# A third k-tile pair by the seven-product scheme, with its weight sums moved from VectorE to GpSimd

## The chip, the cores and the metric

One NeuronCore of a Trainium2 chip runs the kernel. The metric is the device time of one execution in microseconds (us), given as the median of several runs; lower is better. Engines are named as in the profile: PE is TensorE, DVE is VectorE, ACT is ScalarE, POOL is GpSimd, SP is SyncE, which here only issues DMAs.

## What is computed

One layer of a hybrid encoder, on 256 tokens with a model width of 2048, all in float32. Only the two feed-forward blocks (width 5632) are touched by the change:

```
h = h + 1/2 * ((silu(u @ w_gate) * (u @ w_up)) @ w_down),   u = rms_norm(h)
```

One stands ahead of the attention part and one behind it. Between them lie a combined projection, a forgetting attention, a gated linear attention, a merge and an output projection; at the end come a per-layer embedding and a last norm. The weights are far larger than the activations, so every weight is read once and streamed.

## The kernel before

**Precision.** Each float32 matrix is split into a high part (rounded by ACT with a copy, the fp32r type) and a low part (raw minus high, by DVE). A product is three matmuls: high x high, high x low, low x high (`product`, L1511). Each matmul is 128x128 activations against 128x512 weights.

**Phases.** Each feed-forward block is cut into an "a" and a "b" half: `up1a`, `down1a`, `up1b`, `down1b` for the first, `up2a`, `down2a`, `up2b`, `down2b` for the second. The phase before `up2a` is `out`. In an up phase the work goes by column pairs (a stage for each, `pair`): 256 hidden columns of gate beside 256 of up in each of two 512-column tiles. A stage has the 2048 rows of k as 16 k-tiles, taken two at a time: 8 units. `UPS` (L47) gives the pairs of each phase: 5, 5, 6 and 5 stages.

**Items.** A unit done plainly is an item of kind S: 2 column tiles x 2 k-tiles x 2 token tiles x 3 = 24 matmuls. The first `US` = 2 units of a pair (but not of a phase's first pair) are done by Winograd's form of the seven-product scheme: on the 2x2 blocks of the unit, 7 products instead of 8. Four of them (kind A, 12 matmuls) are made in the stage of the pair before, three (kind B, 9 matmuls) in the pair's own stage. Between A and B the banks are combined: ACT copies two banks (`copy_parts`, L632), DVE makes four additions (`combine`, L1072), and PE waits for `combined` before the stage (L1555).

The scheme needs sums of activations (`make_sums`, L1082, once for each feed-forward block, in the first stage of the "a" half) and four sums of weight tiles for every A item: `make_steps` (L1062), on DVE:

```
q[1] = q[2] - q[0];  q[2] = b[1] - q[2];  q[3] = b[1] - q[1];  b[2] = b[0] - q[3]
```

Each is 128x512 with both inputs in SBUF. `q` is the raw buffer of the A item (four tiles, one "quad"), `b` the "trio" that holds the rest of the unit until its B item in the next stage.

**Buffers and order.** There are `QUADS` = 3 raw quads, 3 high and 3 low quads. `stage_of` (L58) writes out the order of a stage:

```
own = [("B", pair, 0), own[US], ("B", pair, 1), *own[US + 1:]]      # L62
own = [*own[:-2], *later, *own[-2:]]                                 # L65
```

so B0 S2 B1 S3 S4 S5 A0 A1 S6 S7. `item_tables` (L108) works out for each item the count at which its buffers are free. SP issues the loads in that order (L393 to L403): it waits on `lo_split` for the raw quad, then issues 1 MB for an S item, or two loads of 512 KB for an A item, with a wait for the trio between them. ACT makes the high part (`split_item`, L620) after a wait for the load (or for `steps_made`) and for PE's item three before (`quad_free`); DVE makes the low part (L1053); PE multiplies (`multiply_item`, L1517). Every engine works in its own program order, and after certain items the engines do other work: the silu and the products of the last pair after the second item (k == 1), their turns into rows after the third on PE and the fifth on ACT and DVE.

One raw quad lies in `more(name)`: for `up2a` and `up2b` in the space of `x_both`, which the phase before `up2a` still reads. So SP waits for the whole `out` phase at L392 before it issues any load of `up2a`.

**POOL** makes constants at the start, the roots of the norms (`root`, L455), small DMAs and, in the merge phase, `bias_scores` (L510): two additions, 128x128 and 128x256, with both inputs in SBUF, for each of eight heads. It does nothing in the feed-forward blocks but the roots.

Of the kernel before, what the change touches and what calls it, by code (L numbers as in the profile page):

```python
# [8 lines left out]
P = 128  # L9
# [6 lines left out]
TOK = 256  # L16
# [33 lines left out]
US = 2  # L50
# [92 lines left out]
def build(nc, x, x_turned, all_gains, p, ffn1_up, ffn1_w_down, w_in,  # L143
# [36 lines left out]
    with ExitStack() as ctx:  # L180
# [29 lines left out]
        room, room_r = shared(("room", [P, 9, COLS], F32), ("room_r", [P, 9, COLS], F32R))  # L210
# [4 lines left out]
        later_in_chunk = sb("later_in_chunk", [P, P])  # L215
        up_to = sb("up_to", [P, P])
        ones = sb("ones", [P, P])
        causal = sb("causal", [P, 3 * P])
# [13 lines left out]
        thin_rows = sb("thin_rows", [P, TOK])  # L232
# [29 lines left out]
        def trio(name, u):  # L262
            return more(name)[0][:, 12:15, :] if u == 0 else room[:, 4:7, :]

        def spare(name):
            return more(name)[0][:, 15, :]

        s_hi = room_r[:, 0:2, :].rearrange("p u (s c) -> p u s c", s=4)
        s_lo = room_r[:, 2:4, :].rearrange("p u (s c) -> p u s c", s=4)
        m1_copy, m5_copy = room[:, 7, :], room[:, 8, :]  # L270
# [32 lines left out]
        steps_made, parts_copied, combined = sem("steps_made"), sem("parts_copied"), sem("combined")  # L303
# [57 lines left out]
        def _(sp):  # L361
# [11 lines left out]
            def feed_forward(up, w_up, first_pair, w_down, kt0, kts):  # L373
# [17 lines left out]
                if up == "up2a":  # L391
                    sp.wait_ge(multiplied, BLOCK[up])  # L392
                for stage in STAGES[up]:  # L393
                    for it in stage:
                        source = w_up[first_pair + it.pair, it.unit]
                        if it.kind != "B" and it.raw_free > 0:
                            sp.wait_ge(lo_split, it.raw_free)
                        if it.kind == "S":
                            sp.dma_start(raw_quad(up, it.raw), source).then_inc(quad_full[it.raw], 16)
                        if it.kind == "A":  # L400
                            sp.dma_start(raw_quad(up, it.raw)[:, 0:3:2, :], source[:, 0:2, :]).then_inc(quad_full[it.raw], 16)
                            sp.wait_ge(lo_split, it.trio_free)
                            sp.dma_start(trio(up, it.unit)[:, 0:2, :], source[:, 2:4, :]).then_inc(trio_full[it.unit], 16)  # L403
# [45 lines left out]
        def _(pool):  # L449
# [9 lines left out]

            nc.gpsimd.memset(ident[:], 0.0).then_inc(pool_chain, 1)  # L460
# [3 lines left out]
            nc.gpsimd.memset(minus_half[:], -0.5).then_inc(ident_ready, 1)  # L464
            nc.gpsimd.memset(ones[:], 1.0).then_inc(pool_chain, 1)
# [16 lines left out]
            root(0)  # L482
            pool.wait_ge(multiplied, BLOCK["down1b"])
# [59 lines left out]
            root(2)  # L543

# [14 lines left out]
        def _(act):  # L559
# [60 lines left out]
            def split_item(name, it):  # L620

                n = 3 if it.kind == "B" else 4
                of = trio(name, it.unit) if it.kind == "B" else raw_quad(name, it.raw)
# [5 lines left out]
                nc.scalar.activation(hi_quad(name, it.quad)[:, 0:n, :], of[:, 0:n, :], ACT.Copy)\  # L629
                    .then_inc(hi_split, item_counts(name, it))  # L630
# [11 lines left out]
            def split_sums(first):  # L642
                for u in range(US):
                    act.wait_ge(sums_made, first + u + 1)
                    nc.scalar.activation(s_hi[:, u, :, :], (m1_copy, m5_copy)[u].rearrange("p (s c) -> p s c", s=4), ACT.Copy)\
# [345 lines left out]
        def _(dve):  # L991
# [61 lines left out]
            def split_item(name, it):  # L1053

                n = 3 if it.kind == "B" else 4
                of = trio(name, it.unit) if it.kind == "B" else raw_quad(name, it.raw)
                dve.wait_ge(hi_split, it.at + 1)
                nc.vector.tensor_tensor(lo_quad(name, it.quad)[:, 0:n, :], of[:, 0:n, :],  # L1058
                                        hi_quad(name, it.quad)[:, 0:n, :].bitcast(F32), ALU.subtract)\
                    .then_inc(lo_split, item_counts(name, it))  # L1060

            def make_steps(name, it):  # L1062

                dve.wait_ge(quad_full[it.raw], 16 * it.raw_count)
                dve.wait_ge(trio_full[it.unit], 16 * it.trio_count)
                q, b = raw_quad(name, it.raw), trio(name, it.unit)
                after_own(nc.vector.tensor_tensor(q[:, 1, :], q[:, 2, :], q[:, 0, :], ALU.subtract))
                nc.vector.tensor_tensor(q[:, 2, :], b[:, 1, :], q[:, 2, :], ALU.subtract)
                after_own(nc.vector.tensor_tensor(q[:, 3, :], b[:, 1, :], q[:, 1, :], ALU.subtract))
                nc.vector.tensor_tensor(b[:, 2, :], b[:, 0, :], q[:, 3, :], ALU.subtract).then_inc(steps_made, 1)  # L1070

            def combine(name, pair):  # L1072
# [3 lines left out]
                u2 = spare(name)  # L1076
                after_own(nc.vector.tensor_tensor(u2, c22[:, :], m1_copy, ALU.add))
                nc.vector.tensor_tensor(c12[:, :], c12[:, :], u2, ALU.add)
                after_own(nc.vector.tensor_tensor(c21[:, :], c21[:, :], u2, ALU.add))
                nc.vector.tensor_tensor(c22[:, :], c21[:, :], m5_copy, ALU.add).then_inc(combined, 1)  # L1080

            def make_sums(name, hi, lo, sums):  # L1082

                for u in range(US):
                    full = spare(name).rearrange("p (k c) -> p k c", k=2)
                    to = (m1_copy, m5_copy)[u].rearrange("p (s c) -> p s c", s=4)
                    pair_of = slice(BK * u, BK * (u + 1))
                    after_own(nc.vector.tensor_tensor(full, hi[:, pair_of, :].bitcast(F32), lo[:, pair_of, :].bitcast(F32), ALU.add))
# [5 lines left out]
                    dve.wait_ge(sums_made, sums + u + 1)  # L1094

            def split_sums(first):
                for u in range(US):
                    dve.wait_ge(sums_hi, first + u + 1)
                    nc.vector.tensor_tensor(s_lo[:, u, :, :], (m1_copy, m5_copy)[u].rearrange("p (s c) -> p s c", s=4),
                                            s_hi[:, u, :, :].bitcast(F32), ALU.subtract).then_inc(sums_lo, 1)  # L1100

            def up_groups(name, kts, sums=None, hi=None, lo=None, first_rows=None, later_rows=None):

                pairs, first = UPS[name]
                for n, stage in enumerate(STAGES[name]):
                    pair = first + n
                    for k, it in enumerate(stage):
                        if k + 1 < len(stage) and stage[k + 1].kind == "A":
                            make_steps(name, stage[k + 1])
                        split_item(name, it)  # L1110
                        if k == 0 and n == 0 and first_rows:
                            first_rows()
                        if k == 1 and pair > 0:
                            hidden_out(name, pair - 1)
                        if k == 1 and n == 0:
                            if later_rows:
                                later_rows()
# [809 lines left out]
```

## Time and profile before

| | |
|---|---|
| Median of 3 runs | 2248.66 us (2248.65 to 2249.57) |
| Profiled execution | 2249.12 us, of which the span from first to last instruction is 2247.1 us |
| Mean granted clock of PE | 0.995 |
| Busy | PE 99%, DVE 60%, ACT 47%, POOL 2% |
| DMA | 425.66 MB, mean 189 GB/s |

The profile lists a matmul with about 0.39 us, but matmuls are pipelined: the distance between two starts is what one costs. A group's line gives busy time and the mean of one instruction. An idle time in brackets is that just before the instruction, with what ended it. "L1058" is the line of the kernel.

### The profile page before, as it was taken

The numbers are of one execution on the slowest core, as the hardware profiler recorded it, in microseconds if no ns is written. First come the engines' busy times: TensorE is split into PE (matmuls) and PEld (weight loads), VectorE is DVE, ScalarE is ACT, GpSimd is POOL, SyncE is SP. The second block draws the span as 40 slices with busy tenths as digits, with TensorE's granted clock in tenths as the row PEclk, the third lists the DMA queues.
The fourth block names the chain that finished last, engine by engine and source line by source line (L and its number), as shares of the span: only waits on it lengthen the run. The fifth ranks groups of instructions, "written<-read, shape, count | busy, mean of one in ns | idle before, by whom it ended". The sixth has DMA issues, their size and how long they took to land.

```text
span 2247.1 us, 24310 instructions
## 1 busy us (share of the span) xinstructions
PE 2217.0 (99%) x9950; PEld 1827.4 (81%) x9950; DVE 1337.5 (60%) x1318; ACT 1050.7 (47%) x1147; POOL 40.4 (2%) x71
## 2 busy tenths in 40 slices
PE   8999999999999999999999998899999999999998
PEld 7888888888888888877778887788878888888886
DVE  5777544677555444445655654777754467755555
ACT  6445434454444444464444443454543345544454
POOL 0000000000010000010000000000000000000000
PEclk9999999999999999999999999999999999999999
DMA  8455456555465666665655664555546664556654
GB/s 312 177 202 205 164 196 205 207 186 191 175 201 187 198 195 190 175 179 173 174 168 159 187 187 143 213 172 203 207 149 191 204 221 171 197 178 212 187 189 147
DMA packets 161079, 425.66 MB, mean 189 GB/s; under 512 B 11320, under 2 KB 11328, under 8 KB 143568
## 3 DMA queue, kind: packets, MB, share of 16 engines
q1 hardware_dynamic: 159216, 419.21, 57.3%
q0 software_dynamic: 1472, 4.70, 0.8%
q8 instruction: 74, 1.21, 0.2%
q10 hardware_dynamic: 288, 0.30, 0.0%
q14 instruction: 29, 0.24, 0.0%
HBM read 422.06 MB, written 2.11 MB: 189 GB/s over the span
## 4 chain that ended last, share of the span: by engine, by line
PE 97%; DMA 1%; DVE 1%; ACT 0%; issue 0%; ACTq 0%; POOLq 0%; POOL 0%
PE acc L1470 18%; PE acc L1472 18%; PE acc L1471 18%; PE acc L1513 6%; PE acc L1515 6%; PE acc L1514 6%; PE turn L1515 4%; PE turn L1513 4%; PE turn L1514 4%; PE fox L1515 4%; PE fox L1514 4%; PE fox L1513 4%; DMA raw<-in_ffn_up 1%; PE turn L1490 1%; PE acc L1507 0%; PE turn L1762 0%
## 5 line engine op out<-in xcount | busy, mean ns | idle before, releaser
L1003 DVE TENSOR_TENSOR w_lo<-raw,w_hi 128x1024 fp32r<-128x1024 f32 x451 | 557.9, 1240 | 604.0 <-ACT w_hi L573 603.6
L573 ACT ACTIVATE w_hi<-raw 128x1024 fp32r<-128x1024 f32 x451 | 477.0, 1060 | 704.0 <-PE acc L1472 633.9
L1470 PE MATMUL acc<-w_hi,x_both 128*128 128x512 f32 x940 | 370.7, 394 | 2.8 <-DVE x_both L1165 2.8
L1472 PE MATMUL acc<-w_hi,x_both 128*128 128x512 f32 x940 | 366.3, 390 | 0.0
L1471 PE MATMUL acc<-w_lo,x_both 128*128 128x512 f32 x940 | 365.9, 389 | 0.0
L1470 PE MATMUL acc<-w_hi,slab_r 128*128 128x512 f32 x832 | 325.9, 392 | 2.6 <-DVE w_lo L1003 2.6
L1472 PE MATMUL acc<-w_hi,slab_r 128*128 128x512 f32 x832 | 324.5, 390 | 0.0
L1471 PE MATMUL acc<-w_lo,slab_r 128*128 128x512 f32 x832 | 324.4, 390 | 0.0
L1058 DVE TENSOR_TENSOR w_lo<-raw,w_hi 128x2048 fp32r<-128x2048 f32 x84 | 192.2, 2290 | 100.8 <-ACT w_hi L629 100.3
L629 ACT ACTIVATE w_hi<-raw 128x2048 fp32r<-128x2048 f32 x84 | 161.2, 1919 | 191.1 <-PE fox L1515 93.5
L1470 PEld LDWEIGHTS acc<-w_hi,x_both 128*128 128x128 f32 x940 | 176.5, 188 | 44.8 <-issue 5.7
L1472 PEld LDWEIGHTS acc<-w_hi,x_both 128*128 128x128 f32 x940 | 176.4, 188 | 37.5
L1471 PEld LDWEIGHTS acc<-w_lo,x_both 128*128 128x128 f32 x940 | 176.6, 188 | 35.3
L1470 PEld LDWEIGHTS acc<-w_hi,slab_r 128*128 128x128 f32 x832 | 156.6, 188 | 34.9 <-issue 2.9
L1472 PEld LDWEIGHTS acc<-w_hi,slab_r 128*128 128x128 f32 x832 | 156.6, 188 | 32.8
L1471 PEld LDWEIGHTS acc<-w_lo,slab_r 128*128 128x128 f32 x832 | 156.5, 188 | 32.2
L1058 DVE TENSOR_TENSOR w_lo<-more,w_hi 128x2048 fp32r<-128x2048 f32 (+1 forms) x41 | 87.4, 2132 | 46.4 <-ACT w_hi L629 46.3
L629 ACT ACTIVATE w_hi<-more 128x2048 fp32r<-128x2048 f32 (+1 forms) x41 | 73.5, 1794 | 72.5 <-PE fox L1515 36.6
L629 ACT ACTIVATE more_r<-more 128x2048 fp32r<-128x2048 f32 (+1 forms) x34 | 63.1, 1856 | 53.9 <-PE acc L1515 30.0
L1058 DVE TENSOR_TENSOR more_r<-more,more_r 128x2048 fp32r<-128x2048 f32 (+1 forms) x34 | 75.2, 2211 | 20.2 <-ACT more_r L629 20.0
L1513 PE MATMUL acc<-w_hi,y_r 128*128 128x512 f32 x183 | 72.9, 398 | 9.3 <-DVE w_lo L1058 9.3
L1058 DVE TENSOR_TENSOR more_r<-raw,more_r 128x2048 fp32r<-128x2048 f32 x26 | 59.5, 2290 | 28.0 <-ACT more_r L629 27.9
(368 smaller groups left out, 3200.9 us busy)
## 6 DMA issues: line engine op xcount, KB each, us to landing
raw<-in_ffn_up SPq DMA_DIRECT2D x88, 1024.0 KB, 4.9
raw<-in_ffn_w_down SPq DMA_DIRECT2D x176, 512.0 KB
raw<-in_w_in SPq DMA_DIRECT2D x96, 512.0 KB
more<-in_ffn_up SPq DMA_DIRECT2D x46, 1024.0 KB, 4.9
raw<-in_w_merge_gate SPq DMA_DIRECT2D x64, 512.0 KB
raw<-in_ffn_up SPq DMA_DIRECT2D x37, 512.0 KB, 4.0
raw<-in_w_out SPq DMA_DIRECT2D x32, 512.0 KB
raw<-in_w_ple_gate SPq DMA_DIRECT2D x32, 512.0 KB
```

Source lines behind the costliest of these rows:

```text
L573: nc.scalar.activation(w_hi[:, slot, :, :], raw[:, slot, :, :], ACT.Copy).then_inc(hi_split, 1)
L629: nc.scalar.activation(hi_quad(name, it.quad)[:, 0:n, :], of[:, 0:n, :], ACT.Copy)\
L1003: nc.vector.tensor_tensor(w_lo[:, slot, :, :], raw[:, slot, :, :], w_hi[:, slot, :, :].bitcast(F32), ALU.subtract).then_inc(lo_split, 1)
L1058: nc.vector.tensor_tensor(lo_quad(name, it.quad)[:, 0:n, :], of[:, 0:n, :], hi_quad(name, it.quad)[:, 0:n, :].bitcast(F32), ALU.subtract)\
L1470: nc.tensor.matmul(to, hi(kt)[:, tok], w_hi[:, slot, k, :], start=kt == 0, stop=False)
L1471: nc.tensor.matmul(to, hi(kt)[:, tok], w_lo[:, slot, k, :], start=False, stop=False)
L1472: last = nc.tensor.matmul(to, lo(kt)[:, tok], w_hi[:, slot, k, :], start=False, stop=kt == BK * nb - 1)
L1490: last = nc.tensor.transpose(turn_bank[bank][:, at:at + P], tile(k, tok), ident[:])
L1513: nc.tensor.matmul(to, x, w, start=start, stop=False, skip_group_check=primed)
L1514: nc.tensor.matmul(to, x, w_rest, start=False, stop=False, skip_group_check=primed)
L1515: return nc.tensor.matmul(to, x_rest, w, start=False, stop=stop, skip_group_check=primed)
```

## The change

- `US` goes from 2 to 3, so three of eight units of a pair are done with seven products, in 17 pairs.
- The order of a stage becomes B0 S3 B1 S4 A0 B2 S5 A1 S6 A2 S7, and in a phase's first stage S0 S1 S2 S3 A0 S4 S5 A1 S6 A2 S7.
- `make_steps` moves from DVE to POOL, which waits for its own results by a semaphore; POOL runs through all A items of two phases (`all_steps`). The making of constants moves behind `up1b`, and the trio of the third unit uses the space of constants ("corner"), so its B item is split in two instructions on ACT and on DVE.
- `make_sums` and `split_sums` use one buffer for the sums of all three units, so that a unit's sums are split before the next one's are made; they come after the third item (k == 2).
- `copy_parts` and `combine` move from the end of a stage to behind the first item of the next one.
- SP's wait for the end of `out` moves to the third item of `up2a`.

```diff
-US = 2
+US = 3
@@ stage_of
-        own = [("B", pair, 0), own[US], ("B", pair, 1), *own[US + 1:]]
+        b0, b1, b2 = [("B", pair, u) for u in range(US)]
+        own = [b0, own[US], b1, own[US + 1], b2, *own[US + 2:]]
     if pair + 1 < pairs:
-        later = [("A", pair + 1, u) for u in range(US)]
-        own = [*own[:-2], *later, *own[-2:]]
+        a0, a1, a2 = [("A", pair + 1, u) for u in range(US)]
+        own = [*own[:4], a0, *own[4:6], a1, own[6], a2, own[7]]
@@ build
+        corner = sb("corner", [P, 2 * COLS])
-            return more(name)[0][:, 12:15, :] if u == 0 else room[:, 4:7, :]
+            return more(name)[0][:, 12:15, :] if u == 0 else room[:, 8:11, :]
+        def later_tiles(name, u):
+            if u < 2:
+                return (trio(name, u),)
+            return corner.rearrange("p (a c) -> p a c", a=2), more(name)[0][:, 15:16, :]
-        m1_copy, m5_copy = room[:, 7, :], room[:, 8, :]
+        m1_copy, m5_copy = room[:, 6, :], room[:, 7, :]
@@ SP
-                if up == "up2a":
-                    sp.wait_ge(multiplied, BLOCK[up])
                 for stage in STAGES[up]:
                     for it in stage:
+                        if up == "up2a" and it.at == BLOCK[up] + 2:
+                            sp.wait_ge(multiplied, BLOCK[up])
@@ POOL
+            def after_step(ins):
+                steps[0] += 1
+                ins.then_inc(step_chain, 1)
+                pool.wait_ge(step_chain, steps[0])
+            def make_steps(name, it):
+                pool.wait_ge(quad_full[it.raw], 16 * it.raw_count)
+                pool.wait_ge(trio_full[it.unit], 16 * it.trio_count)
+                q, later = raw_quad(name, it.raw), later_tiles(name, it.unit)
+                w21, w22 = later[0][:, 0, :], later[0][:, 1, :]
+                t4 = later[0][:, 2, :] if len(later) == 1 else later[1][:, 0, :]
+                after_step(nc.gpsimd.tensor_tensor(q[:, 1, :], q[:, 2, :], q[:, 0, :], ALU.subtract))
+                nc.gpsimd.tensor_tensor(q[:, 2, :], w22, q[:, 2, :], ALU.subtract)
+                after_step(nc.gpsimd.tensor_tensor(q[:, 3, :], w22, q[:, 1, :], ALU.subtract))
+                nc.gpsimd.tensor_tensor(t4, w21, q[:, 3, :], ALU.subtract).then_inc(steps_made, 1)
...
+            root(0)
+            all_steps("up1a")
+            all_steps("up1b")
+            pool.wait_ge(multiplied, BLOCK["down1b"])
             nc.gpsimd.memset(ones[:], 1.0).then_inc(pool_chain, 1)
...
             root(2)
+            all_steps("up2a")
+            all_steps("up2b")
@@ ACT, up_phase
                         split_item(name, it)
+                        if k == 0 and n > 0:
+                            copy_parts(name, pair)
...
-                        if k == 3 and n == 0 and sums is not None:
+                        if k == 2 and n == 0 and sums is not None:
                             split_sums(sums)
...
-                    if pair + 1 < pairs:
-                        copy_parts(name, pair + 1)
@@ DVE
             def combine(name, pair):
-                u2 = spare(name)
-                after_own(nc.vector.tensor_tensor(u2, c22[:, :], m1_copy, ALU.add))
+                after_own(nc.vector.tensor_tensor(m1_copy, c22[:, :], m1_copy, ALU.add))
...
             def make_sums(hi, lo, first):
                 for u in range(US):
+                    full = m5_copy.rearrange("p (k c) -> p k c", k=2)
+                    to = m1_copy.rearrange("p (s c) -> p s c", s=4)
...
                     nc.vector.tensor_tensor(to[:, 3, :], a12, to[:, 1, :], ALU.subtract).then_inc(sums_made, 1)
                     dve.wait_ge(sums_hi, first + u + 1)
+                    nc.vector.tensor_tensor(s_lo[:, u, :, :], to, s_hi[:, u, :, :].bitcast(F32), ALU.subtract)\
+                        .then_inc(sums_lo, 1)
+                    dve.wait_ge(sums_lo, first + u + 1)
@@ DVE, up_groups
-                        if k + 1 < len(stage) and stage[k + 1].kind == "A":
-                            make_steps(name, stage[k + 1])
                         split_item(name, it)
+                        if k == 0 and n > 0:
+                            combine(name, pair)
...
-                            if sums is not None:
-                                make_sums(name, hi, lo, sums)
-                        if k == 3 and n == 0 and sums is not None:
-                            split_sums(sums)
+                        if k == 2 and n == 0 and sums is not None:
+                            make_sums(hi, lo, sums)
...
-                    if pair + 1 < pairs:
-                        combine(name, pair + 1)
```

## Rows read from the trace of the kernel before

**Rows 1.** The page, part 1: busy us of each engine (share) and instructions.
```profile
PE 2217.0 (99%) x9950; PEld 1827.4 (81%) x9950; DVE 1337.5 (60%) x1318; ACT 1050.7 (47%) x1147; POOL 40.4 (2%) x71
```

**Rows 2.** Waits of PE, whole span: us in total, times, longest.
```profile
PE acc L1513 <- DVE w_lo L1058: 9.3, 1, 9.3
PE acc L1513 <- DVE more_r L1058: 3.0, 1, 3.0
...
PE acc L1470 <- DVE w_lo L1003: 2.6, 1, 2.6
```

**Rows 3.** Timeline of one S item: PE's first matmul, the next item's, ACT after it.
```profile
401.99 0.39 PE L1513 MATMUL turn<-more_r,x_both 128*128 128x512 f32 x1
...
407.43 0.39 PE L1513 MATMUL turn<-w_hi,x_both 128*128 128x512 f32 x1
...
407.69 1.92 ACT L629 ACTIVATE more_r<-more 128x2048 fp32r<-128x2048 f32 x1 [3.52 <-PE fox L1515]
```

**Rows 4.** Chain that ended last: the turns of stages two apart (start, us).
```profile
1560.16 0.87 PE acc L1507 x8
1646.30 0.87 PE acc L1507 x8
```

**Rows 5.** Groups by form, ACT and DVE: busy us, mean ns, idle before.
```profile
L629 ACT ACTIVATE w_hi<-raw 128x2048 fp32r<-128x2048 f32 x84 | 161.2, 1919 | 191.1 <-PE fox L1515 93.5 <-PE acc L1515 64.3 <-DMA raw<-in_ffn_up 15.3
...
L1058 DVE TENSOR_TENSOR w_lo<-raw,w_hi 128x2048 fp32r<-128x2048 f32 x84 | 192.2, 2290 | 100.8 <-ACT w_hi L629 100.3
```

**Rows 6.** SP's timeline at an A load, and landing times of its second half (L403).
```profile
1957.25 0.38 SPq L401 DMA_DIRECT2D raw<-in_ffn_up  x1
1957.67 0.47 SPq L403 DMA_DIRECT2D room<-in_ffn_up  x1
...
DMA to landing us min/median/max: 4.6/4.9/6.1
```

**Rows 7.** Chain that ended last at the start of up2a (start, us).
```profile
1398.84 4.96 DMA raw<-in_ffn_up
...
1408.11 0.79 PE acc L1513
```

**Rows 8.** Windows: busy of PE, PEld, DVE, ACT, POOL; PEclk; DMA share; GB/s.
```profile
1408.00:1416.00 8.00, 7.89 (x22) 6.24 (x23) 3.45 (x4) 1.56 (x5) 0.00 (x0) 0.60 0.81 263
1423.00:1432.00 9.00, 6.02 (x27) 4.88 (x27) 8.54 (x8) 2.48 (x3) 0.00 (x0) 1.00 0.54 174
1672.00:1684.00 12.00, 9.45 (x35) 7.34 (x34) 7.43 (x9) 6.42 (x9) 0.00 (x0) 0.86 0.46 151
```

**Rows 9.** POOL's additions, lines 516 and 517: ns min/median/max.
```profile
L516 POOL TENSOR_TENSOR room<-causal,room x8: 469/474/1359, 974.8 to 1168.5; 128x128 f32<-128x128 f32 x8
...
L517 POOL TENSOR_TENSOR room<-causal,room x8: 734/741/1717, 976.1 to 1168.9; 128x256 f32<-128x256 f32 x8
```

**Rows 10.** Timelines of POOL and DVE where they run together (start, us).
```profile
974.77 1.36 POOL L516 TENSOR_TENSOR room<-causal,room 128x128 f32<-128x128 f32 x1 [2.20 <-DMA room<-cum_rows]
...
978.42 1.72 POOL L517 TENSOR_TENSOR room<-causal,room 128x256 f32<-128x256 f32 x1
...
974.58 1.23 DVE L1003 TENSOR_TENSOR w_lo<-raw,w_hi 128x1024 fp32r<-128x1024 f32 x1 [7.34 <-ACT w_hi L573]
975.73 1.28 DVE L1235 SCALAR_TENSOR_TENSOR gates<-turn,gates 128x512 f32<-128x512 f32 x2
...
1061.21 2.29 DVE L1003 TENSOR_TENSOR w_lo<-raw,w_hi 128x1024 fp32r<-128x1024 f32 x1 [0.53 <-ACT w_hi L573]
...
1062.71 0.57 POOL L507 DMA_DIRECT2D room<-cum_rows  x1 [0.30 <-POOL room L517]
```

**Rows 11.** Timelines of DVE and ACT: one unit's sums of activations.
```profile
1419.94 0.69 DVE L1088 TENSOR_TENSOR more<-y_r 128x512 f32<-128x512 f32 x1
...
1421.52 0.29 DVE L1093 TENSOR_TENSOR room<-more,room 128x128 f32<-128x128 f32 x1
...
1423.75 0.63 ACT L645 ACTIVATE room_r<-room 128x512 fp32r<-128x512 f32 x1 [0.83 <-DVE room L1093]
```

More of the change, by code:

```diff
@@ L214, in build @@
         ident = sb("ident", [P, P])
[L215 to L218, printed above, removed]
+        causal, up_to = corner[:, 0:3 * P], corner[:, 3 * P:4 * P]
+        later_in_chunk, ones, thin_rows = corner[:, 4 * P:5 * P], corner[:, 5 * P:6 * P], corner[:, 6 * P:8 * P]
         in_chunk = sb("in_chunk", [P, 2])
@@ L231, in build @@
         forget_bias = sb("forget_bias", [P, HEADS])
-        thin_rows = sb("thin_rows", [P, TOK])
         thin_z = sb("thin_z", [P, TT, 2 * THIN_FOX])
@@ L262, in trio @@
         def trio(name, u):
-            return more(name)[0][:, 12:15, :] if u == 0 else room[:, 4:7, :]
[L265 to L269, printed above, removed]
-        m1_copy, m5_copy = room[:, 7, :], room[:, 8, :]
+            return more(name)[0][:, 12:15, :] if u == 0 else room[:, 8:11, :]
[3 more added lines that the diff above has]
+            return corner.rearrange("p (a c) -> p a c", a=2), more(name)[0][:, 15:16, :]
+        s_hi = room_r[:, 0:3, :].rearrange("p u (s c) -> p u s c", s=4)
+        s_lo = room_r[:, 3:6, :].rearrange("p u (s c) -> p u s c", s=4)
+        m1_copy, m5_copy = room[:, 6, :], room[:, 7, :]
         x_t = slab[:, SLABS - KD:, :, :].rearrange("p k t c -> p k (t c)")
@@ L458, in root, with all_steps @@
                 nc.gpsimd.tensor_tensor(rstd[:], meansq[:], minus_half[:], ALU.pow).then_inc(rstd_done, 1)
+            steps = [0]
+            def after_step(ins):
[12 more added lines that the diff above has]
+                nc.gpsimd.tensor_tensor(t4, w21, q[:, 3, :], ALU.subtract).then_inc(steps_made, 1)
+            def all_steps(name):
+                for stage in STAGES[name]:
+                    for it in stage:
+                        if it.kind == "A":
+                            make_steps(name, it)
             nc.gpsimd.memset(ident[:], 0.0).then_inc(pool_chain, 1)
@@ L620, in split_item @@
             def split_item(name, it):
-                n = 3 if it.kind == "B" else 4
-                of = trio(name, it.unit) if it.kind == "B" else raw_quad(name, it.raw)
                 if it.kind == "S":
@@ L628, in split_item @@
                 act.wait_ge(multiplied, it.quad_free)
-                nc.scalar.activation(hi_quad(name, it.quad)[:, 0:n, :], of[:, 0:n, :], ACT.Copy)\
-                    .then_inc(hi_split, item_counts(name, it))
+                at = 0
+                for of in later_tiles(name, it.unit) if it.kind == "B" else (raw_quad(name, it.raw),):
+                    n = of.shape[1]
+                    last = nc.scalar.activation(hi_quad(name, it.quad)[:, at:at + n, :], of, ACT.Copy)
+                    at += n
+                last.then_inc(hi_split, item_counts(name, it))
             def copy_parts(name, pair):
@@ L644, in split_sums @@
                     act.wait_ge(sums_made, first + u + 1)
-                    nc.scalar.activation(s_hi[:, u, :, :], (m1_copy, m5_copy)[u].rearrange("p (s c) -> p s c", s=4), ACT.Copy)\
+                    nc.scalar.activation(s_hi[:, u, :, :], m1_copy.rearrange("p (s c) -> p s c", s=4), ACT.Copy)\
                         .then_inc(sums_hi, 1)
@@ L1053, in split_item @@
             def split_item(name, it):
-                n = 3 if it.kind == "B" else 4
-                of = trio(name, it.unit) if it.kind == "B" else raw_quad(name, it.raw)
                 dve.wait_ge(hi_split, it.at + 1)
[L1058 to L1070, printed above, removed]
+                at = 0
+                for of in later_tiles(name, it.unit) if it.kind == "B" else (raw_quad(name, it.raw),):
+                    n = of.shape[1]
+                    last = nc.vector.tensor_tensor(lo_quad(name, it.quad)[:, at:at + n, :], of,
+                                                   hi_quad(name, it.quad)[:, at:at + n, :].bitcast(F32), ALU.subtract)
+                    at += n
+                last.then_inc(lo_split, item_counts(name, it))
             def combine(name, pair):
@@ L1075, in combine, with make_sums @@
                 c11, c21, c12, c22 = banks_of(name, pair)
-                u2 = spare(name)
-                after_own(nc.vector.tensor_tensor(u2, c22[:, :], m1_copy, ALU.add))
-                nc.vector.tensor_tensor(c12[:, :], c12[:, :], u2, ALU.add)
-                after_own(nc.vector.tensor_tensor(c21[:, :], c21[:, :], u2, ALU.add))
+                after_own(nc.vector.tensor_tensor(m1_copy, c22[:, :], m1_copy, ALU.add))
+                nc.vector.tensor_tensor(c12[:, :], c12[:, :], m1_copy, ALU.add)
+                after_own(nc.vector.tensor_tensor(c21[:, :], c21[:, :], m1_copy, ALU.add))
                 nc.vector.tensor_tensor(c22[:, :], c21[:, :], m5_copy, ALU.add).then_inc(combined, 1)
-            def make_sums(name, hi, lo, sums):
+            def make_sums(hi, lo, first):
                 for u in range(US):
[L1085 to L1088, printed above, removed]
+                    full = m5_copy.rearrange("p (k c) -> p k c", k=2)
+                    to = m1_copy.rearrange("p (s c) -> p s c", s=4)
+                    kts = slice(BK * u, BK * (u + 1))
+                    after_own(nc.vector.tensor_tensor(full, hi[:, kts, :].bitcast(F32), lo[:, kts, :].bitcast(F32), ALU.add))
                     a11, a21, a12, a22 = full[:, 0, 0:P], full[:, 0, P:], full[:, 1, 0:P], full[:, 1, P:]
```

18 lines of the change are left out of this document (5 added, 13 removed).

## The prediction

> **What bounds the kernel now.** The page's busy row says PE 99% [rows 1]; DVE is at 60%, ACT at 47% and POOL at 2%. A busy share alone does not say that PE sets the end, so the next view is PE's waits [rows 2]: after the start-up the list holds 9.3, 3.0 and 2.6 us and nothing else. PE is therefore the bound everywhere, and a saved matmul is saved time as long as nothing comes late. The timeline gives the price: the 24 matmuls of an S item run from 401.99 to 407.43, 5.44 us, so 226.7 ns each [rows 3]; an A item (12) takes 2.72 us, a B item (9) 2.04 us. A check: the turns of two stages lie 86.14 us apart over two stages [rows 4], 43.07 us each, and 6 S + 2 A + 2 B + 0.87 us of turns is 43.03. So the stages of before have no stall at all.
>
> **What keeps them free of stalls** is a loop of latencies. There are three split buffers. ACT can begin an item's high part when PE has finished the item three before it (PE's item ends at 407.43, ACT starts at 407.69), takes 1.92 us, DVE takes 2.29 us for the low part [rows 3, 5], so the item is ready 4.5 us after that end. Raw buffers are also three: an item's load starts at the low part of the third loaded item before it. An A load is two DMAs 0.42 us apart, the second landing 4.9 us after its issue [rows 6]: 5.3 us.
>
> **The change, part by part.** (a) *Products.* A third unit in each of 17 column pairs (4+4+5+4) takes 21 matmuls for 24: 51 x 0.2267 = **-11.6 us**. A stage with A and B becomes 5 S + 3 A + 3 B + 0.87 = 42.35 us.
>
> (b) *Early loads of up2a.* SP now waits for the end of "out" before the third load only. Before, the first load is issued at 1398.84 and PE starts at 1408.1: 9.3 us idle, then a stretch at mean granted clock 0.60 for 8 us (between the 2.4 and the 1.2 GHz level), 3.2 us lost; then 3.0 us at the third item [rows 2, 7, 8]. The 2.6 us at the next hand-over (down2a's first block, whose raw slot the last item held) goes too, since 63 items end on the third buffer, and with it 14% of 12 us, 1.7 us [rows 2, 8]. Together **-19.8 us**, if nothing new stands there.
>
> (c) *Steps to POOL.* 34 x 4 DVE subtractions of 128x512 (0.69 us for one of this size [rows 11]) go, 51 x 4 POOL ones come. POOL takes 0.47 us for 128x128 and 0.74 us for 128x256 [rows 9], so 0.267 us per 128 columns and **1.28 us for 128x512**, extrapolated. Each of two waits on its own result costs 0.30 us [rows 10]. A unit's four steps: 1.28 + 0.30 + 1.23 + 1.28 + 0.30 + 1.28 = 5.7 us, where DVE took 2.7.
>
> (d) *POOL and DVE together.* The rows show that they hold each other up. The DVE split of 1.24 us takes 2.29 us when POOL's two additions run beside it; and the 0.47 us addition that meets a running split takes 1.36 us, the 0.74 us one 1.72 us [rows 10, 9]. Both sides read two SBUF operands. Two DVE operations with one input in PSUM, at 975.73, kept 0.64 us each beside POOL [rows 10], so combine, silu products and turns are taken to be free of it. I take turns, first come first served, with POOL holding for all but 0.15 us of its operation. The Trainium skill's "SBUF — State Buffer" (Who interferes with whom) states that such a pair is exclusive for the whole instruction; with that last 0.15 us held too, the sum below would be 10 us higher, and it speaks against this change as a whole. By that rule, the trace agrees on the exclusion (2.29 us for 1.24), not on the last tenths of it.
>
> (e) *One middle stage walked through*, 13 of which exist; times in us from B0's start. PE's order without stalls ends B0 2.0, S3 7.5, B1 9.5, turns 10.4, S4 15.8, A0 18.6, B2 20.6, S5 26.0, A1 28.8, S6 34.2, A2 36.9, S7 42.4. A0's second half needs the tile that B0's low part frees at -4.4, so it lands at 0.8; its steps end at 7.7 because B1's low part comes between, and S4's low part ends at 9.8. That frees A1's load, landing 15.15; steps 15.15 to 16.4 and 16.7 to 19.1. S5's high part can't start before S4's end (15.8), is ready at 18.0, its low part waits for POOL until 19.1 and ends at 21.4; PE wanted it at 20.6: **0.8**. POOL's fourth step waits for that low part, ends at 22.6; A1's low part ends at 26.8, just in time. A2's load, freed at 21.4, lands at 26.7; its first step goes ahead of S6's low part, which ends at 30.1 instead of 29.0: **0.6**. That low part in turn holds POOL's steps two and three until 30.0; step four ends at 34.1, high part 36.05, low part 38.35; PE is ready at 35.6: **2.8**. Sum 4.1 x 13 = **+54 us**. Without any exclusion only A2 is late: S5 ready 20.3, load 25.7, steps 31.3, split 35.6 against 34.2: 1.4 us.
>
> (f) *First stages.* The three sums of activations now share one copy buffer, so each waits for ACT and back: 1.87 us to the fifth operation's end, 0.63 us ACT, 0.69 us DVE and the waits, 3.4 us [rows 11], 10.2 us in a row, with S3's split behind them on ACT and DVE. In up1a they begin 4.5 us after the phase and S3's low part ends 1.9 us late, with A0's four steps on POOL in between 6.5. In up2a the third item needs the last row turns and is ready at 12.0; S3's is ready 7.6 us late, with POOL's steps 12.3. A1 and S6 of these two stages add 2.5 each, 0.2 for the third item; up1b and up2b lose 2.7 + 0.6 each. Together 9.0 + 14.9 + 3.3 + 3.3 = **+30.4 us**.
>
> (g) *Clock.* Short idles can drop it: the 2.6 us one did, the 3.0 us one did not [rows 8, 2]. For 15 stalls of about 2.8 us I take half of 1.7, 12.8 us (bounds 0 and 25); after up2a's 12.3 us the same 3.2 as before, after up1a's 6.5 some 2.5. **+18.5 us**.
>
> (h) *At nothing*: 17 more ACT and DVE instructions, since B2 is split in two (it has 5 us of room); the copies and combine, now one S item (5.44 us) before their use instead of two: 0.26 + 2 x 0.63 + 4 x 0.69 + 0.4 of waits = 4.7 us [rows 3, 11], 0.7 to spare, and one operand in PSUM; if they slip, every stage start slips. POOL's constants and thin loads move behind up1b; the constants are used 390 us later. POOL's root for up2a stays ahead of the steps there.
>
> **Sum**: -11.6 - 19.8 + 54 + 30.4 + 18.5 = **+71 us**. The profiled execution took 2249.1 us (span 2247.1), 0.4 above the median of 2248.7. **Forecast 2320 us.** Bounds: a POOL step at 1.2 instead of 1.28 us takes 9 off, at 1.35 adds 13, the clock -13 to +12.
>
> **Rivals.** *No exclusion* (8 in 100): POOL reads beside DVE. Then (e) is 13 x 1.4 = 17.8, (f) 1.9 + 7.6, clock 3.2: -11.6 - 19.8 + 17.8 + 9.5 + 3.2 = -1, **2248 us**, no change. The lengthened rows speak against it. *Faster* (5 in 100): in addition a unit's steps take under 4.3 us, that is below 0.94 us per 128x512 step; A2 is then in time, and the gain is that sum without its 17.8, -19: **2230 us**. For it: nothing but that 128x512 was never seen. *Worse* (9 in 100): DVE's queue of splits wins POOL's place more often or a step takes 1.5 us, the A2 stalls double and each drops the clock: +42 and +12, **2374 us**, against the first-come rows. *The change does not do what it says*: excluded for the products, which are counted out by the item lists; the first two up2a loads still wait for raw slots, but DVE frees these about 14 and 8 us before PE ends "out" (four slots of 2.72 us, a low part 2.6 us after its slot is free). The forecast (78 in 100) has its own range 2288 to 2355.
>
> **Range and chances.** 2265 to 2355 leaves out the faster case, no exclusion and the upper end of worse, near 2 in 10. A measurement can tell 0.2%, 4.5 us. Slower 0.90, within 0.2% 0.05, faster 0.05.
>
> **What the profile would show.** PE's waits: some 40 on DVE low parts of split items, A2's (the last A of a stage) at 2.8 us, turns of middle stages 46.5 us apart (42.4 if there are none); POOL 128x512 rows with a minimum near 1.28 us and a mean well above; DVE's 128x2048 splits lengthened from 2.29 to above 3.3 us where POOL runs; the first up2a item without its 9.3 us; a wait of 12 us at its fourth. Wrong, if POOL's rows and the DVE splits keep their minimum throughout, or if PE's waits name ACT or combine.

## The result and the profile after

| | before | after |
|---|---|---|
| Median | 2249.11 us (2248.65 to 2250.51, 4 runs) | 2320.12 us (2319.02 to 2321.19, 4 runs) |
| Ratio, 95% interval | | 1.0315 (1.0297 to 1.0332) |
| Span of the profiled execution | 2247.1 us | 2319.4 us |
| Mean granted clock of PE | 0.995 | 0.986 |

The kernel became 3.2% slower, 71 us; 2320 had been forecast. The sum was right to a microsecond, which is partly luck: its idle time was about 6 us too high and its clock about 6 us too low.

Busy times and the chain that ended last, from the page of the changed kernel (they answer to [rows 1]), and below them the chain of the kernel before:

```profile
PE 2238.3 (97%) x9899; PEld 1829.4 (79%) x9899; DVE 1341.9 (58%) x1228; ACT 1071.8 (46%) x1183; POOL 447.6 (19%) x275
...
PE 79%; DVE 6%; POOL 6%; DMA 5%; ACT 4%; issue 1%; SPq 0%; ACTq 0%; POOLq 0%; DVEq 0%
...
PE 97%; DMA 1%; DVE 1%; ACT 0%; issue 0%; ACTq 0%; POOLq 0%; POOL 0%
```

PE has 51 matmuls fewer (9899 for 9950), as counted, but it now sets only 79% of the chain, where it set 97%. The busy shares alone would mislead: PE still shows 97%. DVE has 90 instructions fewer than before, and yet its busy time did not fall (1341.9 us for 1337.5): part of what it has left takes longer, as the splits below show.

PE's waits in the changed kernel, with total us, times and the longest one (they answer to [rows 2]):

```profile
PE acc L1530 <- DVE w_lo L1093: 26.0, 14, 11.6
PE turn L1530 <- DVE more_r L1093: 19.9, 8, 7.4
PE turn L1530 <- DVE w_lo L1093: 13.9, 11, 3.1
PE acc L1530 <- DVE more_r L1093: 7.9, 8, 3.1
```

That is 67.7 us in 41 waits, all for the low part of a split item; before there were three such waits with 14.9 us. The longest, 11.6 us, is at the fourth item of `up2a`; 7.4 us is the same place in `up1a`. The other lines of PE's list are start-up waits, 4.0 us in all, where it had 6.0 before.

One middle stage on PE's timeline, from the A2 before it to its own A2:

```profile
519.02 0.80 PE L1530 MATMUL turn<-w_hi,x_both 128*128 128x512 f32 x1 [2.30 <-DVE w_lo L1093]
...
549.93 0.50 PE L1530 MATMUL turn<-w_hi,x_both 128*128 128x512 f32 x1 [0.28 <-DVE w_lo L1093]
558.65 0.50 PE L1530 MATMUL turn<-more_r,x_both 128*128 128x512 f32 x1 [0.26 <-DVE more_r L1093]
566.69 0.79 PE L1530 MATMUL acc<-w_hi,x_both 128*128 128x512 f32 x1 [2.30 <-DVE w_lo L1093]
```

The brackets give the idle time. The three waits stand where the prediction's walk had put them: at S5 (0.3 us), S6 (0.3) and A2 (2.3). From A2 to A2 it is 47.7 us, against 43.07 before [rows 4] and 42.35 without waits.

The chain that ended last, through the load and the steps of that A2:

```profile
550.33 4.68 DMA corner<-in_ffn_up
...
555.13 1.32 POOL raw L477
556.46 0.07 issue
556.52 3.22 POOL raw L478
559.74 1.26 POOL raw L479
561.00 0.07 issue
561.07 1.30 POOL more L480
562.37 0.02 issue
562.39 1.93 ACT w_hi L662
564.32 0.02 issue
564.34 2.30 DVE w_lo L1093
566.64 0.04 issue
566.69 0.79 PE acc L1530
```

Load, four steps, high part, low part, product: one after another, 16.4 us. Three POOL steps take 1.3 us; the second takes 3.22. Beside it runs the split of the item before, which takes 3.38 us instead of 2.29:

```profile
555.21 3.38 DVE L1093 TENSOR_TENSOR more_r<-more,more_r 128x2048 fp32r<-128x2048 f32 x1
```

POOL's steps and DVE's splits by duration (ns: minimum/median/maximum), from the view of single lines:

```profile
L477 POOL TENSOR_TENSOR raw<-raw x35: 1285/1439/3297, 59.7 to 2029.6; 128x512 f32<-128x512 f32 x35
...
L480 POOL TENSOR_TENSOR room<-room,raw x13: 1285/3215/3222, 93.2 to 2034.9; 128x512 f32<-128x512 f32 x13
...
L1093 DVE TENSOR_TENSOR w_lo<-raw,w_hi x93: 2279/2292/3407, 50.7 to 2082.1; 128x2048 fp32r<-128x2048 f32 x93
```

The minimum of POOL's 128x512 step is 1.285 us, where 1.28 had been extrapolated from the two smaller additions of [rows 9]. The maximum adds 1.9 to 2.0 us, most of a DVE split; the split's own maximum is 3.41 us for 2.28, most of a POOL step more. Each engine waits for the other, as in [rows 10]. Of the 168 splits of 128x2048, 41 are stretched, by 36 us in sum. A unit's four steps take POOL 5.6 to 10.6 us, 8.1 in the mean, where four plain steps and two waits would make 5.3.

Windows of 8 us behind four stalls (busy of PE, PEld, DVE, ACT, POOL; then PEclk, DMA share, GB/s), which answer to [rows 8]:

```profile
566.60:574.60 8.00, 7.91 (x28) 6.42 (x29) 5.99 (x7) 3.77 (x4) 0.00 (x0) 0.79 0.73 261
1548.00:1556.00 8.00, 8.00 (x35) 6.65 (x36) 7.58 (x7) 3.69 (x4) 0.00 (x0) 1.00 0.78 262
1594.40:1602.40 8.00, 8.00 (x29) 6.51 (x30) 6.14 (x6) 3.68 (x4) 0.00 (x0) 0.81 0.76 262
1468.80:1476.80 8.00, 7.97 (x23) 6.35 (x24) 4.37 (x2) 1.18 (x1) 0.00 (x0) 0.64 0.86 267
```

Behind 12 of the 13 A2 stalls of middle stages, each of 2.3 to 3.1 us, the mean granted clock is near 0.8 over 8 us, so about 1.6 us more are lost; the exception is the one at 1548, which with 3.09 us was among the longest. The 2.3 us stall at A2 in the first stage of `up1a` lowered nothing either. PE keeps its busy share in these windows and makes 28 or 29 matmuls instead of 35. The fourth window is the start behind the 11.6 us wait.

### The profile page after: what moved, and what is told of

Read it like the earlier page. It is cut to its first block, busy times and chain, and to the rows that moved or that the text cites. A ratio compares the mean times of both kernels' runs of the same rounds, so it can differ in the third digit from the quotient of the medians.

```text
span 2319.4 us, 24392 instructions
## 1 busy us (share of the span) xinstructions
PE 2238.3 (97%) x9899; PEld 1829.4 (79%) x9899; DVE 1341.9 (58%) x1228; ACT 1071.8 (46%) x1183; POOL 447.6 (19%) x275
## 3 DMA queue, kind: packets, MB, share of 16 engines
q8 instruction: 74, 1.21, 0.2%
## 4 chain that ended last, share of the span: by engine, by line
PE 79%; DVE 6%; POOL 6%; DMA 5%; ACT 4%; issue 1%; SPq 0%; ACTq 0%; POOLq 0%; DVEq 0%
PE acc L1487 17%; PE acc L1489 17%; PE acc L1488 17%; DMA corner<-in_ffn_up 3%; PE acc L1530 3%; PE acc L1532 3%; PE acc L1531 3%; DVE w_lo L1093 3%; PE turn L1530 3%; PE turn L1532 2%; PE turn L1531 2%; PE fox L1530 2%; PE fox L1531 2%; PE fox L1532 2%; ACT w_hi L662 2%; DVE more_r L1093 2%
## 5 line engine op out<-in xcount | busy, mean ns | idle before, releaser
L1093 DVE TENSOR_TENSOR w_lo<-raw,w_hi 128x2048 fp32r<-128x2048 f32 x93 | 231.3, 2503 | 171.5 <-ACT w_hi L662 171.3
L662 ACT ACTIVATE w_hi<-raw 128x2048 fp32r<-128x2048 f32 x93 | 176.2, 1911 | 231.0 <-POOL more L480 102.3
L477 POOL TENSOR_TENSOR raw<-raw 128x512 f32<-128x512 f32 x35 | 67.0, 1915 | 653.5 <-DMA more<-in_ffn_up 510.3
L1093 DVE TENSOR_TENSOR more_r<-more,more_r 128x2048 fp32r<-128x2048 f32 (+2 forms) x54 | 118.6, 2197 | 80.6 <-ACT more_r L662 80.6
L662 ACT ACTIVATE more_r<-more 128x2048 fp32r<-128x2048 f32 (+2 forms) x54 | 90.6, 1679 | 108.0 <-POOL more L480 59.1
L1530 PE MATMUL acc<-w_hi,y_r 128*128 128x512 f32 x166 | 67.1, 404 | 19.0 <-DVE w_lo L1093 19.0
L1093 DVE TENSOR_TENSOR w_lo<-more,w_hi 128x2048 fp32r<-128x2048 f32 (+2 forms) x38 | 78.9, 2075 | 10.1 <-ACT w_hi L662 9.9
```

The costliest lines, as they stand in the source:

```text
L477: after_step(nc.gpsimd.tensor_tensor(q[:, 1, :], q[:, 2, :], q[:, 0, :], ALU.subtract))
L662: last = nc.scalar.activation(hi_quad(name, it.quad)[:, at:at + n, :], of, ACT.Copy)
L1093: last = nc.vector.tensor_tensor(lo_quad(name, it.quad)[:, at:at + n, :], of, hi_quad(name, it.quad)[:, at:at + n, :].bitcast(F32), ALU.su ...
L1530: nc.tensor.matmul(to, x, w, start=start, stop=False, skip_group_check=primed)
```

## The experiments

The theory: POOL's steps are long, and they take turns with DVE's splits, since both read SBUF; that makes the last A item of each stage late. The rivals: POOL's length alone; the new order or the later combine; something else in the change. The kernel before ran beside every experiment, and each ratio is to that.

### Early loads alone, in the kernel before

```diff
-                if up == "up2a":
-                    sp.wait_ge(multiplied, BLOCK[up])
                 for stage in STAGES[up]:
                     for it in stage:
+                        if up == "up2a" and it.at == BLOCK[up] + 2:
+                            sp.wait_ge(multiplied, BLOCK[up])
```

> The kernel of before with one part of the change alone: SP waits for the end of the out phase at the third load of up2a instead of the first. Theory (the 9.3 us wait and the half clock after it come from the late first load, and the 3.0 us wait goes with them): PE's 9.3 us wait is gone, the third item waits 0 to 3 us, the 2.6 us wait at down2a stays because the item list is the old one; time 2233 to 2241 us. Rival (another operand of the first item is as late as the load, the wait only changes its name): 2246 us or more.

Measured: 2237.15 us, ratio 0.9945 (0.9929 to 0.9962). PE's waits in it:

```profile
PE acc L1513 <- DVE more_r L1058: 3.0, 1, 3.0
PE acc L1470 <- DVE w_lo L1003: 2.6, 1, 2.6
```

The 9.3 us wait is gone: 12 us, the gain that this part of the change has by itself. The rival falls. The 3.0 and 2.6 us waits are still there, but the lowered clock has changed places: it now stands behind the 3.0 us wait, which had none in the kernel before, and no longer behind the 2.6 us one. The two windows:

```profile
1412.90:1420.90 8.00, 7.96 (x22) 6.32 (x23) 5.59 (x4) 0.12 (x1) 0.00 (x0) 0.61 0.83 292
1666.60:1674.60 8.00, 7.96 (x39) 6.74 (x40) 6.05 (x8) 5.00 (x9) 0.00 (x0) 1.00 0.78 257
```

### Late loads again, in the changed kernel

The same lines the other way round, put into the changed kernel.

> The changed kernel with one part undone: SP waits for the end of the out phase before the first load of up2a again. Theory (the early loads take 9.3 us away at up2a's start, but the wait behind the sums stays and follows, so less is seen here than in the kernel of before with early loads alone): the 9.3 us wait is back, the third item no longer waits, the fourth still waits some 11 us, each long wait with its half clock; time 8 to 13 us above the changed kernel, 2328 to 2334 us. Rival (the sums' wait merely takes the place of the load's wait): within 4 us of the changed kernel.

Measured: 2330.03 us, ratio 1.0358 (1.0341 to 1.0376), so some 10 us above the changed kernel (ratio 1.0315). The 9.3 us wait is back, and the 11.6 us wait at the fourth item stands as before, so the rival falls. The part does pay in the changed kernel too, and hides there under the loss of the rest.

### The steps back on DVE

```diff
-            all_steps("up1a")
-            all_steps("up1b")
...
-            all_steps("up2a")
-            all_steps("up2b")
...
+                        if k + 1 < len(stage) and stage[k + 1].kind == "A":
+                            make_steps(name, stage[k + 1])
                         split_item(name, it)
```

with `make_steps` on DVE, as before, for three units; all else as changed.

> The changed kernel with the weight steps put back on DVE and all else as changed (three units, the new order, one buffer for the sums, early loads). Theory (POOL's slower steps and their taking turns with DVE's splits make most of the 71 us): the last A of a stage still waits, 1.5 to 2.5 us, the others hardly; time 2258 to 2272 us. Rival (the order of the items, or combine with one item of room, makes the loss): 2300 us or more.

Measured: 2266.26 us, ratio 1.0073 (1.0056 to 1.0089); 54 us of the 71 go with the move to POOL. But the kernel is still slower than before. The largest of its waits:

```profile
PE acc L1540 <- DVE w_lo L1089: 21.9, 9, 9.0
PE turn L1540 <- DVE more_r L1089: 12.1, 6, 4.7
```

So part of the loss is not POOL's. The size of the stall is as expected, but the late item is another one: in each of the 13 middle stages PE waits 1.5 to 3.4 us at S6, the plain item ahead of A2, and never at A2. DVE and PE in one such stage:

```profile
582.08 0.69 DVE L1101 TENSOR_TENSOR more<-more 128x512 f32<-128x512 f32 x1 [2.48 <-DMA corner<-in_ffn_up]
...
584.75 2.28 DVE L1089 TENSOR_TENSOR w_lo<-raw,w_hi 128x2048 fp32r<-128x2048 f32 x1
...
587.09 0.50 PE L1540 MATMUL acc<-w_hi,x_both 128*128 128x512 f32 x1 [1.60 <-DVE w_lo L1089]
```

In DVE's program A2's steps stand ahead of S6's split. DVE waits there for A2's load (2.48 us idle), makes the steps, and only then splits S6. So an item that needs no steps is held up by the steps of the next one.

### POOL writes only, for about as long as plain steps

```diff
-                after_step(nc.gpsimd.tensor_tensor(q[:, 1, :], q[:, 2, :], q[:, 0, :], ALU.subtract))
-                nc.gpsimd.tensor_tensor(q[:, 2, :], w22, q[:, 2, :], ALU.subtract)
-                after_step(nc.gpsimd.tensor_tensor(q[:, 3, :], w22, q[:, 1, :], ALU.subtract))
-                nc.gpsimd.tensor_tensor(t4, w21, q[:, 3, :], ALU.subtract).then_inc(steps_made, 1)
+                flat = q[:, :, :].rearrange("p k c -> p (k c)")
+                for n in range(3):
+                    after_step(nc.gpsimd.memset(flat[:, 512:2048 - 210], 0.0))
+                nc.gpsimd.memset(flat[:, 1248:2048], 0.0)
+                nc.gpsimd.memset(t4, 0.0).then_inc(steps_made, 1)
```

> The changed kernel with POOL's four steps of a unit replaced by memsets of about the same total length (some 5.7 us with their waits), so POOL reads no SBUF; the weight sums are left out. Theory (the exclusion is between DVE operations with two SBUF inputs and POOL operations that read SBUF): DVE's splits keep 2.29 us, POOL's memsets keep their length, only the last A of a stage waits, about 1.4 us; time 2246 to 2262 us. Rival 1 (POOL's length alone makes the loss): within 15 us of the changed kernel, 2305 or more. Rival 2 (writes exclude as well): also 2305 or more, with splits lengthened.

Measured: 2245.48 us (10 runs), ratio 0.9987 (0.9978 to 0.9997). One of POOL's groups, by form (busy us, mean ns), and DVE's splits by duration:

```profile
L479 POOL MEMSET raw<- 128x1326 f32 x105 | 126.9, 1209 | 702.5 <-DMA more<-in_ffn_up 510.4 <-DMA room<-in_ffn_up 122.8 <-DMA corner<-in_ffn_up 65.3
...
L1094 DVE TENSOR_TENSOR w_lo<-raw,w_hi x93: 2279/2291/2295, 50.2 to 2006.2; 128x2048 fp32r<-128x2048 f32 x93
```

The unit takes POOL 5.04 us (3 x 1.21, 0.77, 0.53 and the waits). That is near the 5.3 us of four plain steps and well below the 8.1 us that they took in the changed kernel. 75 us of the changed kernel's time are gone, and no split is longer than 2.295 us. So POOL's plain length is not the loss; that it reads SBUF for so long is. The time came out half a microsecond below the range: the last A item waited 0.3 to 0.6 us in 11 of 13 middle stages, less than the 1.4 us of the walk without exclusion, which had counted on 5.7 us for a unit.

### POOL writes shortly

The four steps as memsets of 128x512.

> The changed kernel with POOL's steps as memsets of 128x512, about 0.53 us each, 2.7 us for a unit; the weight sums are left out. Theory: no A item waits, what is left is the wait behind the sums of activations in up1a (about 2 us) and up2a (about 8 us); time 2230 to 2241 us. This is what the change would give if the steps cost nothing. Rival (something else in the change, such as combine or the order, also holds PE): above 2250 us.

Measured: 2232.06 us, ratio 0.9924 (0.9907 to 0.9940). Its waits on split items are these two:

```profile
PE acc L1530 <- DVE w_lo L1093: 7.5, 1, 7.5
PE turn L1530 <- DVE more_r L1093: 3.2, 1, 3.2
```

Nothing waits in a middle stage, so combine with one item of room and B2 in two instructions cost nothing. The two waits stand behind the sums of activations. A unit takes POOL 2.16 us here; the difference to the long memsets, 13 us, is what 2.9 us more for a unit cost without the exclusion.

### POOL reads one input

The four subtractions as copies of 128x512 (`tensor_copy`), the same waits.

> The changed kernel with POOL's subtractions replaced by copies of 128x512, one SBUF input instead of two; the weight sums are left out. Theory A (any POOL operation that reads SBUF takes turns with DVE's two-input splits): some DVE splits are lengthened by up to the length of a copy, and copies that meet a split take up to 2.3 us more; time 2236 to 2262 us, above the short memsets. Theory B (only POOL operations with two inputs take turns): splits keep 2.29 us, time within 4 us of the short memsets (2232).

Measured: 2236.45 us, ratio 0.9942 (0.9926 to 0.9957), its interval overlapping that of the short memsets. The time does not decide; the durations do:

```profile
L480 POOL COPY room<-room x17: 616/617/2753, 89.1 to 1952.3; 128x512 f32<-128x512 f32 x17
...
L1093 DVE TENSOR_TENSOR more_r<-more,more_r x54: 681/2291/2729, 47.2 to 1999.0; 128x2048 fp32r<-128x2048 f32 x41, 128x512 fp32r<-128x512 f32 x8, 128x1536 fp32r<-128x1536 f32 x5
```

A copy of 0.62 us takes up to 2.75 us, and a split of 2.29 us up to 2.73, though only two of 168 splits are clearly stretched (2.70 and 2.73 us). One input is enough for taking turns (theory A), but the copies are so short that it costs little. Copies as long as the subtractions were not tried. The Trainium skill's "SBUF — State Buffer" (Who interferes with whom) states this: a DVE operation with two SBUF inputs contends with a GpSimd operation that reads SBUF, and not with one that only writes. The three runs agree with it: beside subtractions 41 splits are longer than 2.4 us, beside copies 2, beside memsets none.

### A better order, steps on DVE

```diff
-        own = [b0, own[US], b1, own[US + 1], b2, *own[US + 2:]]
+        own = [b0, own[US], b1, own[US + 1], own[US + 2], b2, *own[US + 3:]]
...
-        own = [*own[:4], a0, *own[4:6], a1, own[6], a2, own[7]]
+        own = [*own[:5], a0, *own[5:7], a1, a2, own[7]]
```

on top of the steps on DVE.

> Three units with seven products, weight steps on DVE, and the order of a middle stage changed to B0 S3 B1 S4 S5 A0 B2 S6 A1 A2 S7 (B0 S3 B1 S4 A0 B2 S5 A1 S6 A2 S7 in the change). Theory (an A item waits because its load is freed by the low part of an item that itself comes just in time behind two short ones; here no S item stands behind A and B together before A2's load): no waits in middle stages, only those behind the sums of activations, about 2 and 7.5 us; time 2226 to 2236 us, some 33 us below the same steps in the order of the change. Rival (DVE's load of splits and steps is the cause of the waits there, whatever the order): 2255 us or more.

Measured: 2233.04 us, ratio 0.9929 (0.9915 to 0.9942), 33 us below the same steps in the order of the change. Its waits on split items:

```profile
PE acc L1540 <- DVE w_lo L1089: 7.5, 1, 7.5
PE turn L1540 <- DVE more_r L1089: 3.2, 1, 3.2
```

The middle stages are free of waits. In the order of the change S5 stands behind A0 and B2, together 4.8 us, against the 4.5 us that its own split needs, so its low part is only just in time, and A2's load hangs on it. From there the load (5.1 us), A2's steps (2.8) and S6's split (2.3) make 10.1 us, while PE has S5 and A1 to do, 8.2 us; the rest is the wait at S6. In the better order A2's raw quad is freed by A0's low part and its trio by B2's, and neither is late: in the stage from 499.35 the load has landed at 522.6, and PE comes to A2 at 533.6. The kernel is faster than before, and does all of the computation.

### The better order with the steps on POOL

The same two lines on top of the changed kernel.

> The changed kernel, steps on POOL, with the order B0 S3 B1 S4 S5 A0 B2 S6 A1 A2 S7 alone. Theory (POOL's 5.7 us for a unit and its turns with DVE need room between A items, and here A1 and A2 stand together, so POOL's steps for A2 come behind those for A1): the waits at A2 grow to 3 to 4 us, the total is 2322 to 2345 us. Rival (the order is better whoever makes the steps): below 2310 us.

Measured: 2345.09 us, ratio 1.0421 (1.0405 to 1.0437), just past the upper edge of what was expected and 25 us worse than the change. Its two largest waits:

```profile
PE acc L1530 <- DVE w_lo L1093: 27.0, 7, 11.1
PE turn L1530 <- DVE more_r L1093: 22.9, 6, 7.2
```

In 12 of the 13 middle stages PE waits 3.7 to 3.8 us at A2. The order that suits DVE is the worse one for POOL: A1 and A2 stand together, and POOL makes one unit behind the other. Of the two orders, the change had the better one for its own engine.

### Sums of activations apart

On top of the better order with the steps on DVE: each unit's sums go where their low part will lie (`room[:, 3 + u, :]`), and the three units are spread over three items.

```diff
-                        if k == 2 and n == 0 and sums is not None:
-                            make_sums(hi, lo, sums)
+                        if n == 0 and sums is not None and 3 <= k < 3 + US:
+                            split_sum(k - 3, sums)
+                        if n == 0 and sums is not None and 2 <= k < 2 + US:
+                            make_sum(k - 2, hi, lo)
```

> As the order experiment, and the sums of activations of each unit in a place of their own (where their low part comes to lie), one unit made after the third, fourth and fifth item, each split one item later. Theory (the waits at the fourth item of up1a and up2a come from three sums in a row, each waiting for ACT and back): both go, and the half clock after the longer one; time 2214 to 2225 us. Rival (the late row turns keep the fourth item of up2a waiting anyway): within 4 us of the order experiment.

Measured: **2220.33 us**, ratio 0.9869 (0.9854 to 0.9884), 1.3% faster than before and 4.3% faster than the change. The 7.5 and 3.2 us waits are gone; behind the start-up the list of PE's waits holds one line on a split item:

```profile
PE acc L1544 <- DVE w_lo L1088: 1.1, 1, 1.1
```

## Why the prediction was right, point by point

**Products, (a).** -11.6 us: 51 matmuls fewer are in the page's count. Right.

**Early loads, (b).** -19.8 us. The 9.3, 3.0 and 2.6 us waits are not in the list after, so the sum is right. Alone in the kernel before, the part gave 12 us where 9.3 + 3.2 stood in the sum, and the 3.0 and 2.6 us waits stayed: early loads do not take these away. The 2.6 us one was put down to the longer item list, which was not tried by itself. The 3.0 us one stood behind the sums of activations, which DVE made ahead of the third item's split:

```profile
1423.75 2.29 DVE L1058 TENSOR_TENSOR more_r<-more,more_r 128x2048 fp32r<-128x2048 f32 x1
```

In the change the sums come after that split, and the wait went to the fourth item.

**POOL's step, (c).** 1.28 us extrapolated, 1.285 measured. One detail was off: the wait on POOL's own result was put at 0.30 us; on the chain above it is 0.07. That takes 0.5 us off each unit, 5.7 to 5.3 us without turns.

**Taking turns, (d).** Shown, by the run in which POOL writes for about as long as plain steps and the loss is gone. The rival without exclusion was given 2248 us; that run, which is its experiment, measured 2245.5, with a unit 0.7 us shorter than the rival's. That POOL's reading matters, and not its writing, is told by the memsets and the copies. The longest split is 1.13 us over its plain length, which is a POOL step less 0.15 us, as the walk had it.

**Middle stages, (e).** 54 us forecast, with 0.8, 0.6 and 2.8 in a stage. Measured 0.2 to 0.4 at S5 and S6 and 2.3 at A2, or 0.3 to 0.4 at S5 alone and 3.0 to 3.1 at A2, in sum 41.5 us of idle in 30 waits, and each wait costs about 0.27 us beyond its idle time, since the next matmul comes 0.33 instead of 0.23 us later and the last one's end is counted with 0.39: together near 50. The place and the mechanism were right, the size 4 us too high, which the shorter gap between POOL's steps would explain; that was not tried by itself. As a sign the prediction gave turns 46.5 us apart; 12 of the 13 stages take 47.7 to 48.1 us. The sign left out what the clock (1.7 us) costs in each stage; the one stage without a lowered clock, from 1509.78 to 1556.30, takes 46.5.

**First stages, (f).** 30.4 us forecast; 26.2 us of idle in 11 waits measured, near 29. The long ones were 6.5 and 12.3 in the forecast, 7.4 and 11.6 in the trace. The run with the sums apart confirms their cause. With the steps on DVE in the better order, or with short memsets, they are 3.2 and 7.5, so some 4.2 us of each is POOL's. The forecast had that too, by the steps of A0. The trace also shows the sums themselves stretched: of the first unit's 128x128 operations, which take 0.29 us alone, three take 1.26 to 1.37.

```profile
1453.08 1.26 DVE L1115 TENSOR_TENSOR room<-room 128x128 f32<-128x128 f32 x1
```

**Clock, (g).** This is the term that was mis-sized. Half of 15 stalls were expected to lower the clock, +18.5 us in all, 13.6 net of what the kernel before lost to it. Counted where PE ran at the lowered clock, the loss is 24.3 us against 4.8 before, net 19.5. Of the 24.3, the 12 stalls at A2 make 19.7, where 12.8 stood in the sum; the starts behind 7.4 and 11.6 us make 1.7 and 2.9. (The mean granted clock of the whole span would give 0.014 x 2319 = 32.5 us against 11.2, too much on both sides: part of the lowered clock lies inside the waits and behind the last matmul.) The step that failed was to read one drop and one non-drop as a chance of one half.

**The sum**, from the trace: -11.6 for the products, +52.8 of idle on split items (67.7 - 14.9), +10.3 for 38 more restarts, +19.5 of clock, -2.0 at the start-up: 69.0, against 72.3 between the spans. Some 3 us stay without a name. The forecast had 69.5 us of idle and 13.6 of clock, the trace 63.1 and 19.5; the two errors cancel, which is luck.

**At nothing, (h).** Combine and the split of B2: no wait of PE names combine in any run, and the short memsets have no wait in middle stages. Right.

**Not in the prediction.** Its rivals asked about POOL's reading, its length and its turns with DVE; none asked what the new order costs by itself. With the steps on DVE the order of the change costs 33 us, and that loss stands at S6 and not at the last A item.

## What to carry to other kernels

Here work went to POOL to relieve a DVE that was not the bound. That bought nothing, and since both read SBUF it cost DVE and POOL each other's time; look in the trace of before for any pair that overlapped and compare the stretched durations with the plain ones, eight small operations were enough here. A latency loop must be walked item by item, and in each engine's own program order: an operation sits on the path when its input is freed by something that is itself just in time, or when it stands behind another item's wait. Then the order of the items counts as well as the engine: 33 us for the order, 54 for the engine. A saving of 12 us in matmuls needs every item on time, because a stall of 2.3 us cost about 4 here with the restart and the clock.

## What was not expected of the hardware

Stalls of 2.3 us lowered the granted clock to a mean near 0.8 over the next 8 us in most cases, while one of 3.09 us (at 1548) and one of 3.0 us in the kernel before did not. That same wait of 3.0 us did lower it in the run with early loads alone, to a mean of 0.61 over 8 us, so the length of a stall does not decide; what does was not settled. A POOL operation that waits for its own engine's semaphore begins 0.07 us later, where 0.30 us had been seen ahead of a DMA issue. A POOL copy of 128x512 takes 0.62 us, a two-input subtraction 1.285 us, twice as long.
